# A modulated transformer on one core: a new order of the first loads, narrower causal scores, and an earlier final gain

## The reference

```python
cond = silu(c)
for l in range(DEPTH):                         # DEPTH = 2
    mod = cond @ ada_w[l] + ada_b[l]           # 9 * 1024 columns
    sh1, sc1, g1, sh2, sc2, g2, sh3, sc3, g3 = split(mod, 9)
    h = rms_norm(x, norm_ffn1[l]) * (1 + sc1) + sh1
    x = x + 0.5 * (1 + g1) * swiglu(h, w1, w3, w2)
    h = rms_norm(x, norm_mix[l]) * (1 + sc2) + sh2
    x = x + (1 + g2) * token_mix(h, ...)       # gated delta rule and causal MLA, 8 heads
    h = rms_norm(x, norm_ffn2[l]) * (1 + sc3) + sh3
    x = x + 0.5 * (1 + g3) * swiglu(h, w1, w3, w2)
# causal scores, in blocks of 128 queries:
s = where(kpos <= qpos, q @ k.T * scale, -inf); p = softmax(s); o = p @ v
# second block: mixer, cross-attention to mem, conv_ffn, twice; then
return rms_norm(x, final_norm)
```

## Time and profile before

| | us |
|---|---|
| Median of 3 runs | 2919.12 (2918.94 to 2922.39) |
| The profiled execution | 2922.69 |
| Its span | 2920.9 |
| PE busy | 2776.0 (95%) |
| DVE busy | 1537.2 (53%) |
| ACT busy | 468.8 (16%) |
| Mean granted clock of PE, share of full | 0.983 |

### The profile page before, as it was taken

How to read it: one execution, slowest core, us unless ns; L and a number is a source line. 1 busy time by engine, 2 the same in 40 slices (tenths; PEclk the granted TensorE clock), 3 DMA queues, 4 the chain that set the end, 5 groups by cost and what they waited for, 6 DMA issues and landing times.

```text
span 2920.9 us, 38976 instructions
## 1 busy us (share of the span) xinstructions
PE 2776.0 (95%) x16254; PEld 2491.7 (85%) x16254; DVE 1537.2 (53%) x3064; ACT 468.8 (16%) x823; POOL 104.0 (4%) x88
## 2 busy tenths in 40 slices
PE   3999999999999999999999999997999999988998
PEld 3899889888889999888878999875788997877888
DVE  4458675453447666566553566444235652223565
ACT  1001332320100100242231100113110011111000
POOL 0000000000000330000000230000000000000000
PEclk7999999999999999999999999998999999989999
DMA  7887521234787444331133444421334444322442
GB/s 286 304 298 270 224 101 58 74 114 163 279 301 261 159 172 172 142 119 59 58 116 130 151 168 174 159 101 72 115 115 146 158 159 144 116 100 88 159 148 97
DMA packets 73440, 454.98 MB, mean 156 GB/s; under 512 B 8112, under 2 KB 8880, under 8 KB 27440
## 3 DMA queue, kind: packets, MB, share of 16 engines
q1 hardware_dynamic: 73120, 451.44, 42.4%
q0 software_dynamic: 144, 1.05, 0.1%
HBM read 451.41 MB, written 1.05 MB: 155 GB/s over the span
## 4 chain that ended last, share of the span: by engine, by line
PE 92%; DVE 4%; issue 1%; DMA 1%; DVEq 1%; ACT 0%; SPq 0%; ACTq 0%
PE psum L506 21%; PE psum L460 20%; PE psum L615 14%; PE psum L555 9%; PE psum L754 7%; PE psum L835 4%; PE psum L674 3%; PE psum L698 2%; PE psum L570 2%; PE psum L774 2%; PE psum L686 1%; PE psum L482 1%; PE psum L721 1%; PE psum L711 1%; DMA aring<-astream 1%
## 5 line engine op out<-in xcount | busy, mean ns | idle before, releaser
L460 PE MATMUL psum<-h,ring 128*128 128x256 f32 x1776 | 391.3, 382 | 22.7 <-issue 20.2
L460 PEld LDWEIGHTS psum<-h,ring 128*128 128x128 f32 x1776 | 340.1, 192 | 73.2 <-issue 22.8
L506 PE MATMUL psum<-h,ring 128*128 128x256 f32 x1376 | 299.0, 380 | 29.7 <-ACT h L1054 29.7
L506 PEld LDWEIGHTS psum<-h,ring 128*128 128x128 f32 x1376 | 262.5, 191 | 66.1 <-issue 30.1
L506 PE MATMUL psum<-aring,ring 128*128 128x256 f32 x1408 | 304.7, 379 | 1.7 <-issue 1.7
L506 PEld LDWEIGHTS psum<-aring,ring 128*128 128x128 f32 x1408 | 267.4, 190 | 38.7 <-issue 2.4
L615 PE MATMUL psum<-arena 128*128 128x128 f32 x2112 | 249.6, 275 | 0.0
L615 PEld LDWEIGHTS psum<-arena 128*128 128x128 f32 x2112 | 242.6, 192 | 0.0
L754 PE MATMUL psum<-h,ring 128*128 128x256 f32 x1024 | 232.5, 383 | 0.0
L754 PEld LDWEIGHTS psum<-h,ring 128*128 128x128 f32 x1024 | 194.2, 192 | 27.3 <-issue 1.9
L615 PE MATMUL psum<-arena,ring 128*128 128x128 f32 x1584 | 191.6, 275 | 0.0
(11 more groups left out here) (396 smaller groups left out, 3420.0 us busy)
## 6 DMA issues: line engine op xcount, KB each, us to landing
ring<-wstream SPq DMA_DIRECT2D x354, 1024.0 KB, 4.8
aring<-astream SPq DMA_DIRECT2D x134, 512.0 KB, 4.8
ring<-astream SPq DMA_DIRECT2D x10, 512.0 KB, 13.3
kst<-const SPq DMA_DIRECT2D x1, 1344.5 KB, 10.3
x<-xT SPq DMA_DIRECT2D x1, 1024.0 KB, 7.4
arena<-memT POOLq DMA_DIRECT2D x1, 1024.0 KB, 6.1
outT<-h SPq DMA_DIRECT2D x1, 1024.0 KB, 3.9
condb<-crow SPq DMA_DIRECT2D x1, 512.0 KB, 5.3
```

The lines of the kernel that those rows point to most:

```text
L460: mm = pe.matmul(out, lhsT=tile_at(at[0] % RING, t), rhs=rhs(k), start=k == 0, stop=k == kt - 1)
L506: mm = pe.matmul(psum[:, s % 4, n * T:(n + 1) * T], lhsT=tile_at(slot, n * KD + k), rhs=rhs(k), start=k == 0, stop=k == KD - 1)
```

## The change

SP now issues condb first, then block 0, x, the ones matrix alone (64 KB), and blocks 1 to 15, with `p1` ahead of block 8. All 16 blocks go to places of their own in `arena` (`ada_head`), none into `ring` or `aring`. The slabs of the ring follow without a wait; the rest of `kst`, the positions, `psm` and `p2` come between slabs 0 and 1, and blocks 16 to 18 between slabs 1 and 2. On DVE the sums of blocks 0 to 10 come first (turn -1), then the root of the norm, then x times the root in two products of 1024 columns, then blocks 11 to 15 and the modulation; ACT squares x, and applies scale and shift to each tile in one activation (`first_norm`). In attention, `width` makes the first block of queries work on 128 keys in all kinds but "mem": scores on PE, mask, maximum and scaling on DVE, exponential on ACT; where DVE did both blocks in one instruction of 512 columns it now does one of 128 and one of 256. In the tail, `down` multiplies x by the final gain as each pair of tiles is done, two products of 1024 columns apply the root, and each half is stored as it is ready.

```diff
-HEAD = 2 * RING
-HEAD_ALL = 16
+HEAD = 16
+HEAD_FIRST = 11
-    turn = {b: 0 for b in range(16)}
+    turn = {b: -1 if b < HEAD_FIRST else 0 for b in range(HEAD)}
+        ada_head = [area(b * D + (0 if b < 14 else D), D) for b in range(HEAD)]
+        def width(kind, t):
+            return T if kind == "mem" or t else P
         def _(sp):
+            sp.dma_start(condb[:], crow.broadcast_to((P, D))).then_inc(cond_in, 16)
             for b in range(HEAD):
                 if b == 1:
-                    sp.dma_start(condb[:], crow.broadcast_to((P, D))).then_inc(cond_in, 16)
                     sp.dma_start(x[:], xT).then_inc(norm_inputs_in, 16)
-                    sp.dma_start(kst[:], const).then_inc(norm_inputs_in, 16)
-                sp.dma_start(ring[:, b // 2, b % 2 * D:(b % 2 + 1) * D], astream[b]).then_inc(head_landed[b], 16)
-            for b in range(HEAD, HEAD + AHEAD):
-                sp.dma_start(aring[:, b % AHEAD], astream[b]).then_inc(ada_landed[b % AHEAD], 16)
-            for dst, src in ((p1[:], par1.rearrange("l p n -> p l n")), (psm[:], pars),
-                             (p2[:], par2.rearrange("l p n -> p l n")), (posi, pos.broadcast_to((P, T)))):
-                sp.dma_start(dst, src).then_inc(inputs_in, 16)
+                    sp.dma_start(ones, const[:, 0:P]).then_inc(norm_inputs_in, 16)
+                if b == HEAD // 2:
+                    sp.dma_start(p1[:], par1.rearrange("l p n -> p l n")).then_inc(gains_in, 16)
+                sp.dma_start(ada_head[b], astream[b]).then_inc(head_landed[b], 16)
             b = HEAD + AHEAD
             for i in range(SLABS):
-                if i < RING:
-                    sp.wait_ge(ada_used, 2 * i + 2)
+                if i == 1:
+                    for dst, src in ((kst[:, P:], const[:, P:]), (posi, pos.broadcast_to((P, T))), (psm[:], pars),
+                                     (p2[:], par2.rearrange("l p n -> p l n"))):
+                        sp.dma_start(dst, src).then_inc(inputs_in, 16)
+                if i == 2:
+                    for a in range(HEAD, HEAD + AHEAD):
+                        sp.dma_start(aring[:, a % AHEAD], astream[a]).then_inc(ada_landed[a % AHEAD], 16)
...
-                while i == RING - 1 and b < HEAD_ALL + AHEAD:
-                    sp.wait_ge(ada_used, b - AHEAD + 1)
-                    sp.dma_start(aring[:, b % AHEAD], astream[b]).then_inc(ada_landed[b % AHEAD], 16)
-                    b += 1
-            sp.wait_ge(result_ready, 1)
-            sp.dma_start(outT, h[:]).then_inc(y_out, 16)
-            sp.wait_ge(y_out, 16)
+            for a in range(2):
+                sp.wait_ge(result_ready, a + 1)
+                sp.dma_start(outT[:, 4 * a:4 * a + 4], h[:, 4 * a:4 * a + 4]).then_inc(y_out, 16)
+            sp.wait_ge(y_out, 32)
...
-                                    mm = pe.matmul(psum[:, i % 2 * 2 + m, t * T:(t + 1) * T],
-                                                   lhsT=qs[a][:, t * P:(t + 1) * P], rhs=ks[a],
+                                    w = width(kind, t)
+                                    mm = pe.matmul(psum[:, i % 2 * 2 + m, t * T:t * T + w],
+                                                   lhsT=qs[a][:, t * P:(t + 1) * P], rhs=ks[a][:, 0:w],
...
+            def first_norm():
+                act.wait_ge(norm_inputs_in, 32)
+                E(sq[:], x[:], ACT.Square).then_inc(operands_of_act, 1)
+                norm(KD)
+                act.wait_ge(inputs_for_act, cnt.next("inputs_for_act"))
+                for k in range(KD):
+                    E(h[:, k], h[:, k], ACT.Identity, bias=mods[:, k:k + 1], scale=mulc[:, k:k + 1]
+                      ).then_inc(operands_of_act, 1)
...
-                            STT(out=dst, in0=s, scalar=scale, in1=mask, op0=ALU.mult, op1=ALU.add)
+                        for t in range(2):
+                            w = width(kind, t)
+                            d, k, z = dst[:, t, 0:w], mask[:, t, 0:w], s[:, t, 0:w]
+                            if kind == "mlstm":
+                                TT(d, k, sq[:, i, 0:w], ALU.add)
+                            elif kind == "mla":
+                                STT(out=d, in0=z, scalar=col(RQ, 8 * t + i), in1=k, op0=ALU.mult, op1=ALU.add)
+                            else:
+                                STT(out=d, in0=z, scalar=scale, in1=k, op0=ALU.mult, op1=ALU.add)
                         D()
                         if kind == "fox":
-                            TT(dst, dst, sq[:, i:i + 1].broadcast_to((P, 2, T)), ALU.subtract)
+                            for t in range(2):
+                                w = width(kind, t)
+                                TT(dst[:, t, 0:w], dst[:, t, 0:w], sq[:, i, 0:w], ALU.subtract)
                             D()
-                        V.tensor_reduce(col(MX, b * 4 + 2 * m, 2), dst, AXX, ALU.max)
+                        for t in range(2):
+                            V.tensor_reduce(col(MX, b * 4 + 2 * m + t, 1), dst[:, t, 0:width(kind, t)], AXX, ALU.max)
...
+            ada_sums(-1)
+            root_of_mean(KD * P)
             dve.wait_ge(norm_inputs_in, 32)
-            TT(sq[:], x[:], x[:], ALU.mult).then_inc(operands_of_dve, 1)
+            for a in range(2):
+                TT(h[:, 4 * a:4 * a + 4], x[:, 4 * a:4 * a + 4], both(std[:], 4), ALU.mult)
             ada_sums(0)
+            dve.wait_ge(gains_in, 16)
+            modulation(0, 0)
+            D().then_inc(inputs_for_act, 1)
             dve.wait_ge(inputs_in, 64)
...
-            down(None)
+            down(None, scaled_to=h, gain=lambda k: S("final", k))
             root_of_mean(KD * P)
-            for k in range(KD):
-                scaled(h[:, k], x[:, k], S("final", k), std[:])
-            D().then_inc(result_ready, 1)
+            for a in range(2):
+                v = h[:, 4 * a:4 * a + 4]
+                TT(v, v, both(std[:], 4), ALU.mult).then_inc(result_ready, 1)
```

More of the change, by code:

```diff
@@ L306, in build @@
         freed = {}
+        gains_in = sem("gains_in")
         inputs_in = sem("inputs_in")
@@ L628, in norm_all @@
             def norm_all(kt, sq=sq):
-                pe.wait_ge(operands_of_dve, cnt.next("operands_of_dve"))
+                pe.wait_ge(operands_of_act, cnt.next("operands_of_act"))
                 for k in range(kt):
@@ L1245, in attention @@
                             for t in range(2):
-                                src = LB[:, b, m, t]
+                                dst = src = LB[:, b, m, t, 0:width(kind, t)]
                                 if kind == "mem":
                                     src = psum[:, b * 2, t * T:(t + 1) * T]
-                                last = E(LB[:, b, m, t], src, ACT.Exp, bias=col(NM, b * 4 + m * 2 + t),
+                                last = E(dst, src, ACT.Exp, bias=col(NM, b * 4 + m * 2 + t),
                                          scale=XSCALE if kind == "mem" else 1.0,
@@ L1300, in _ @@
             for layer in range(DEPTH):
-                norm(KD, lambda k: mods[:, k:k + 1], h, layer > 0)
-                if layer == 0:
+                if layer > 0:
+                    norm(KD, lambda k: mods[:, k:k + 1], h, True)
+                else:
+                    first_norm()
                     act.wait_ge(inputs_in, 64)
@@ L1370, in root_of_mean, with norm @@
                 inverse_root(r, m)
-            def norm(src, kt, gain, dst, shifted=True, squared=False):
-                if not squared:
-                    D()
-                    TT(sq[:, 0:kt], src[:, 0:kt], src[:, 0:kt], ALU.mult).then_inc(operands_of_dve, 1)
+            def norm(src, kt, gain, dst, shifted=True):
                 root_of_mean(kt * P)
@@ L1586, in ada_sums @@
                         dve.wait_ge(head_landed[b], 16)
-                        w = ring[:, b // 2, b % 2 * KD * P:(b % 2 + 1) * KD * P]
+                        w = ada_head[b]
                     else:
@@ L1694, in stage @@
                         mask = (K("bmask") if kind == "diff" else K("cmask")).rearrange("p (a t) -> p a t", a=2)
[L1695 to L1702 removed]
+                        for t in range(2):
[5 more added lines that the diff above has]
+                                STT(out=d, in0=z, scalar=col(RQ, 8 * t + i), in1=k, op0=ALU.mult, op1=ALU.add)
+                            else:
+                                STT(out=d, in0=z, scalar=scale, in1=k, op0=ALU.mult, op1=ALU.add)
                         D()
                         if kind == "fox":
[L1705 to L1707 removed]
+                            for t in range(2):
+                                w = width(kind, t)
+                                TT(dst[:, t, 0:w], dst[:, t, 0:w], sq[:, i, 0:w], ALU.subtract)
+                            D()
+                        for t in range(2):
+                            V.tensor_reduce(col(MX, b * 4 + 2 * m + t, 1), dst[:, t, 0:width(kind, t)], AXX, ALU.max)
                     D()
@@ L1732, in normalise @@
```

(23 more changed lines are left out.)

9 lines of the change are left out of this document (1 added, 8 removed).

## The result

The changed kernel takes **2885.73 us**, median of 4 runs (2884.64 to 2887.26), against 2919.09 for the kernel before beside it: a ratio of 0.9883, 95% interval 0.9866 to 0.9901, 33.4 us less. The forecast was 2887.5, 31.6 less. The profiled execution took 2884.82.

What follows compares the result with a forecast made beforehand. TensorE (PE) was taken to bound nearly the whole span, except a head waiting for a late modulation block. Head 15.7, attention 13.8 and tail 2.1 sum to 31.6 us off 2919.12: 2887.5 us, range 2883 to 2897.

Steps and rivals of the forecast that it cites:

- Head, 15.7: Start of the kernel: first feed-forward product at 35.2 us instead of 50.92, 15.7 us sooner.
- The rate: Load queue in the head: arrivals reckoned at 402 KB/us, against a documentation page's 358 GB/s.
- rival C: Behind the head: slabs 1 and 2 come late, cover of 5.7 us used up; 2893 us, chance 0.07.
- MLA, 7.0: MLA attention: narrower scores save 6.7 us on PE, last heads' narrower DVE scaling 0.3; 7.0 together.
- Fox, 3.4: Fox attention: 1.7 us from narrower PE scores plus 0.25 us of DVE wait gone in seven heads; 3.4.
- Diff, 2.4: Differential attention: 1.7 us on PE plus shorter DVE chains in two steps without fill; 2.4 together.
- mLSTM, 1.0: mLSTM heads: narrower scores save 0.8 us, taken as 1.0 because the first scores run at half clock.
- Tail, 2.1: End of the kernel: early final gain and output stored in halves save 2.1 us.
- rival B: Attention: DVE's split instructions cost what they save; 2889.5 us, or 2890.5 if each costs 0.03 more; chance 0.12.
- D: Attention on PE: narrow scores run at the pace of wide ones, losing 10.9 us; 2898.5 us, chance 0.05.
- E: Head: not shorter, because the chain of x, squares and root is longer than read; 2903 us, chance 0.02.
- F: MLA loops: narrower scores let PE's clock fall to 1.2 GHz; slower, 2970 us or so, chance 0.03.

Runs made afterwards that it cites:

- The two repeats: The kernel before and the changed kernel, each run again unedited: 2920.36 us (profiled run) and 2885.98 us.
- the wide scores: The changed kernel with PE making the first block's scores at 256 columns again, DVE and ACT staying narrow: 2897.2 us, ratio 0.9916.
- the head alone: The kernel before with only the new load order, x times root between the sums and ACT's square: 2904.58 us, ratio 0.994.
- the kernel with the root last: The changed kernel without the two products of x and root, the root behind all 16 sums, eight products after the modulation: one run, 2890.79 us.
- the root after sixteen blocks: The changed kernel with all 16 blocks summed ahead of the root instead of 11, products of x kept: one run, 2886.15 us.

## Why the prediction was right, and where it was only near

- **Head, 15.7.** 15.9 in the profile, 15.85 alone. Each step of the sum lies within 0.3: block 10, root, last sum, start (35.2 against 35.01). The rows also show two small misses against each other: ScalarE's eight outputs take 4.06 instead of 3.30, 0.51 a tile instead of 0.41, because each now carries a scale per partition as well as a bias (the Trainium skill, ScalarE: Activation LUTs, gives some 0.09 for each such operand, and the trace agrees); PE follows tile by tile and is slower than that at half clock, so only the first tile's 0.1 counts (0.75 from ScalarE's start to PE's, not 0.65). And the large blocks came 0.1 to 0.3 sooner than the sum has them; the small loads came 0.7 later (DVE's angles wait for the last of them up to 36.54, not 35.8), which cost nothing. Three slips of the prediction change no term: the 16.12 of the earlier trace rows is the time of the transfer, not of DVE's wait; ten blocks go to the ring, not eleven; and its 402 KB/us are KB of 1024 bytes, so 412 GB/s and 3% above the 401 of the window, not the same.
- **The rate.** The rule that I set aside, a limit of some 358 GB/s (the Trainium skill, DMA: Bandwidth & Descriptors, Specifications), is not what this core shows: 419 and 432 in the windows above, 412 over the 32 us of the prediction. The same page's section Bandwidth has 425 for a core measured by itself and gives 358 for when both cores stream; with the 425 the trace agrees within some 3%.
- **The cover behind the head, rival C.** No PE wait at slabs 1 to 4. The angles were ready at 44.23, a second gate at 50.57: as summed.
- **MLA, 7.0.** Lead 3.4 in each layer: 6.8, of which 6.7 is the PE term. At the last head of a layer the lead grows by 0.07 more, 0.14 in all, where the sum had 0.3.
- **Fox, 3.4**: 3.5. **Diff, 2.4**: 2.7 (lead from 26.5 to 29.2). The two waits that DVE ends shrank by 0.48 and 0.55, against 0.50 and 0.26 in the sum: the second term was 0.3 too small.
- **mLSTM, 1.0.** The lead grew by 6.9 here. This is the only term that was far off, and its excess is not the change's columns: the clock rows above price it, 16.0 us fewer at half clock, up to 8 us of PE work. The two repeats show 4.8 from the first scores to the end of the span (436.2 to 431.4), of which 2.0 is the tail and 1.0 the term: 1.8 is left for the clock. The term of 1.0 itself is not shown apart from it; PE's 0.8 is, by the wide scores.
- **Tail, 2.1.** 2.0 in the profile, 1.8 alone.
- **DVE's splits, rival B.** A pair of 128 and 256 is 0.62, of twice 256 it is 0.76. The Trainium skill, VectorE: DVE Perf Modes, on the TRN2 errata, has a formula for one instruction that prices 512 columns right (0.69). Summed without overlap, an estimate, it gives 0.72 and 0.85 for the pairs: the trace does not agree with such a sum.
- **D** fell with the wide scores, **E** with the head alone, **F** with the clock in the loops: 1.00 in after from 607 to 652 (MLA) and from 1910 to 1950 (fox), as in before at the same work (623.5 to 671.6 and 1933 to 1976).

The forecast lies 1.8 above the measured median. The interval of the ratio is worth 10 us, so this remainder has no cause that the runs could show. In the pair of profiled spans the remainder is 6.3, and nearly all of it is the mLSTM stretch.

## What to carry to other kernels

When a late transfer is moved away, ask which engine is last then, and take its optional work out from ahead of the last items: here the products of x, which look free between two sums, cost 2.2 us in front of the last sums and save 0.4 behind them. That is read at the start of the products; in the time of the whole kernel it did not show. Masked-out columns are worth cutting on every engine, but for two separate reasons: on PE wherever PE sets the pace, and on DVE only where DVE's chain ends the step, as in fox. Compare kernels stage by stage at the starts of the same instruction, not span by span, as soon as the granted clock differs between executions.

## What was not expected of the hardware

The time at 1.2 GHz differs between kernels, and between executions of one, by more than some terms of this sum. The mean granted clock of a span, for before, its repeat, and after:

```profile
core 0: 2920.9 us, clock 0.983
```

```profile
core 0: 2918.6 us, clock 0.984
```

```profile
core 0: 2883.0 us, clock 0.988
```

By 2 x (1 - clock) x span these are 99, 93 and 69 us at half speed. Not all of that is lost time, since PE can be idle in it. The idle head accounts for some of it: up to 51 us PE has almost nothing to do before, and between 35 and 51 the clock there was 0.50, while in after, where the first product starts at 35.01, it was 0.91 in the same stretch:

```profile
35.00:51.00 16.00, 0.08 (x1) 0.11 (x1) 6.99 (x16) 0.73 (x2) 0.00 (x0) 0.50 0.92 349
```

```profile
35.00:51.00 16.00, 15.99 (x67) 13.90 (x68) 6.58 (x20) 7.47 (x14) 0.00 (x0) 0.91 0.99 411
```

The rest lies behind short idle stretches of PE, the one ahead of mLSTM above all. The same idle time does not always bring it: ahead of the first fox scores PE waits 2.96 us in after and in the kernel with the root last, and the 16 instructions behind it (line 739) take 3.62 us in after, but 6.40 with the root last.

Thirteen runs of before on one chip spread from 2915.93 to 2924.67, the fastest at a clock of 0.986. Among the head variants with the same attention, the three with 0.988 took 2884.8 to 2886.2 (after, its repeat, and the root after sixteen blocks), and the four with 0.986 or 0.987, first products 1 to 4 us sooner, took 2886.8 to 2890.8 in their profiled runs. So what an earlier start gave, longer half-clock stretches elsewhere took back: in the kernel with the root last, a lead of 1.4 over after at 1809 us is a lag of 3.3 at 1917, behind those instructions. Whether the start shifts the clock in a regular way or this was chance in single runs stays open: three of the four ran once, and all four on another chip than the repeat of after and the root after sixteen blocks. The kernel before took 2919.84 on the one and 2920.52 on the other, so the chip is not seen to matter, but after itself was not run beside these four.
